# Attention scores ahead of the next group's query products on TensorE

## The reference

```
q = (u @ w_qg)[:, :1024] -> (group 4, head 4, token 512, 64) * 64**-0.5
for each block of 128 tokens:
    sc  = q @ kc.T                      # 31 compressed keys
    pc  = masked_softmax(sc)            # over the compressed keys
    ssel = q @ selected keys.T          # 16 >= 8 blocks, so all causal keys
    ps  = masked_softmax(ssel)
    sw  = q @ window keys.T             # window 512, so all causal keys too
    pw  = masked_softmax(sw)
    o   = gate0 * pc @ vc + gate1 * ps @ vs + gate2 * pw @ vw
y = o @ w_o
```

## Time and profile before

| what | value |
|---|---|
| median of 3 runs | 1482.14 us |
| the profiled execution, its time | 1483.61 us |
| the profiled execution, its span | 1481.9 us |
| attention loop on TensorE | about 800.7 to 1035 us of the span |
| PE busy over the span | 1299.8 us (88%) |
| mean granted TensorE clock | 0.935 |

### The profile page before, as it was taken

One profiled execution on the slowest core, in us unless ns is written; L12 is line 12 of the kernel. 1 busy time (PEld: TensorE's weight loads), 2 busy tenths in 40 slices (PEclk: granted clock), 3 DMA queues, 4 the chain that ended last, 5 costly groups with the idle time before them and its releaser, 6 DMA issues.

```text
span 1481.9 us, 18499 instructions
## 1 busy us (share of the span) xinstructions
PE 1299.8 (88%) x6655; PEld 1012.4 (68%) x6655; DVE 1086.3 (73%) x1201; ACT 770.5 (52%) x998; POOL 303.3 (20%) x344
## 2 busy tenths in 40 slices
PE   1399997949999999988989999999985999999985
PEld 0277775747777777747986677675774777777762
DVE  5648683868888888857984666655368888888867
ACT  0322321317777777754443555567142777777760
POOL 3011111421000000026101554445151100000020
PEclk9999998859999999999979999999966999999998
DMA  8657775319999999961621332330623999999972
GB/s 305 235 165 244 268 247 216 128 57 340 404 376 390 394 386 381 387 229 43 219 62 68 103 101 86 100 115 22 226 112 131 386 382 386 384 384 386 392 285 86
DMA packets 107568, 356.07 MB, mean 240 GB/s; under 512 B 8034, under 2 KB 16446, under 8 KB 107470
## 3 DMA queue, kind: packets, MB, share of 16 engines
q1 hardware_dynamic: 82984, 269.52, 48.4%
q0 software_dynamic: 19952, 69.83, 13.6%
q10 hardware_dynamic: 4566, 15.84, 2.6%
HBM read 330.99 MB, written 25.21 MB: 240 GB/s over the span
## 4 chain that ended last, share of the span: by engine, by line
PE 39%; issue 33%; DVE 14%; ACT 6%; DMA 5%; POOL 3%; ACTq 0%; DVEq 0%; POOLq 0%
PE bank L233 8%; PE bank L234 7%; PE bank L235 7%; DVE acc L361 3%; PE bank L1934 2%; PE bank L1952 2%; DMA xg<-scratch_u,tok 2%; POOL prob L2169 2%; PE bank L894 1%; PE bank L1922 1%; ACT w_hi L1107 1%; DMA ada<-in_ada_w_dram 1%; POOL xg L1043 1%; PE bank L1923 1%; DMA rows<-scratch_mods 1%
## 5 line engine op out<-in xcount | busy, mean ns | idle before, releaser
L1113 DVE TENSOR_TENSOR w_lo<-raw,w_hi 128x2048 fp32r<-128x2048 f32 x189 | 436.9, 2316 | 71.6 <-ACT w_hi L1107 71.2
L1107 ACT ACTIVATE w_hi<-raw 128x2048 fp32r<-128x2048 f32 x189 | 362.5, 1919 | 85.6 <-PE bank L235 75.1
L233 PE MATMUL bank<-w_lo,xe_hi 128*128 128x512 f32 x512 | 212.6, 415 | 10.5 <-DVE xe_lo L1070 10.4
L235 PE MATMUL bank<-w_hi,xe_hi 128*128 128x512 f32 x512 | 204.5, 399 | 0.0
L234 PE MATMUL bank<-w_hi,xe_lo 128*128 128x512 f32 x512 | 204.3, 399 | 0.0
L228 DVE TENSOR_TENSOR w_lo<-raw,w_hi 128x2048 fp32r<-128x2048 f32 x37 | 87.1, 2358 | 109.9 <-ACT w_hi L223 109.7
L1043 POOL DMA_INDIRECT xg<-scratch_u,tok x32 | 38.2, 1193 | 555.9 <-DVE tok L1037 555.3
L223 ACT ACTIVATE w_hi<-raw 128x2048 fp32r<-128x2048 f32 x37 | 70.5, 1910 | 134.5 <-PE bank L235 125.7
L233 PE MATMUL bank<-u_lo,w_hi 128*128 128x512 f32 x288 | 119.9, 416 | 11.3 <-DVE q L1839 9.3
L2169 POOL TENSOR_SCALAR prob<-prob,rsum,gates 128x512 f32<-128x512 f32 (+3 forms) x128 | 108.5, 862 | 100.4 <-DVE rsum L2137 100.2
L233 PEld LDWEIGHTS bank<-w_lo,xe_hi 128*128 128x128 f32 x512 | 97.6, 191 | 40.3 <-issue 11.9
(11 more groups left out here) (297 smaller groups left out, 2467.7 us busy)
## 6 DMA issues: line engine op xcount, KB each, us to landing
raw<-in_w_gu_dram SPq DMA_DIRECT2D x128, 1024.0 KB, 8.2
raw<-in_w_down_dram SPq DMA_DIRECT2D x64, 1024.0 KB, 8.6
ada<-in_ada_w_dram POOLq DMA_DIRECT2D x64, 512.0 KB, 5.4
ada<-in_ada_w_dram SPq DMA_DIRECT2D x32, 512.0 KB, 3.8
scratch_y<-ye ACTq DMA_DIRECT2D x30, 512.0 KB, 7.5
raw<-in_conv_w_in_dram SPq DMA_DIRECT2D x12, 1024.0 KB, 9.6
raw<-in_w_kv_dram SPq DMA_DIRECT2D x6, 1024.0 KB, 8.0
rows<-scratch_mods POOLq DMA_DIRECT2D x10, 512.0 KB, 7.7
```

The source lines that it names most:

```text
L233: nc.tensor.matmul(o, lh, rl, start=start, stop=False)
L235: return nc.tensor.matmul(o, lh, rh, start=False, stop=stop)
L1107: nc.scalar.activation(w_hi[:, hslot, :], raw[:, slot, :], ACT.Copy).then_inc(hi_done, 1)
L1113: nc.vector.tensor_tensor(w_lo[:, slot, :], raw[:, slot, :], w_hi[:, hslot, :].bitcast(F32), ALU.subtract).then_inc(lo_done, 1)
```

## The change

In `attention_pe`, the loop over a step's units that calls `scores_pe` moves above the block that calls `q_part_pe`. Nothing else is different; no instruction is added or removed.

```diff
@@ -2032,11 +2032,11 @@
             pe.wait_ge(vcz_made, 1 + GQA)
             for s in range(NS):
                 g, j = divmod(s, NSG)
+                for u in units_of(s):
+                    scores_pe(pe, u)
                 if g + 1 < NKV and j % 5 != 4 and j < 9:
                     for k in range(2):
                         q_part_pe(pe, g + 1, j // 5, 2 * (j % 5) + k)
-                for u in units_of(s):
-                    scores_pe(pe, u)
                 for n, h in mod_half_at(s):
                     mod_half_pe(pe, n, h)
                 if s >= 1:
```

## The result

The changed kernel took 1471.48 us, median of 7 runs (1469.34 to 1475.84). The kernel before had 1482.14 us over 7 runs, those with the change among them (1477.17 to 1487.15). The ratio is 0.9935 with a 95% interval of 0.9915 to 0.9955, so the gain is 9.6 us, between 6.7 and 12.6 (the two medians alone lie 10.7 apart). Forecast were 5.2 us gained and 1476.9 us, with a range down to 1472.9. One later execution of the kernel before was slow, 2544.11 us at a granted clock of 1.00, and is left out of all comparisons.

The account below looks back on a forecast made before the run. TensorE, busy 88% of the span, was taken as the bound in attention except at a few waits. Terms: 4.8 + 2.6 + 0.5 - 2.7 = 5.2 us gained, 1482.14 - 5.2 = 1476.9 us, range 1472.9 to 1480.6.

Parts of the forecast that it names:

- Step 5, the cover: Step 5, groups 0 to 2: scores fill TensorE's wait before the query products, idle 3.1 to about 1.5 us; 4.8 us gained.
- Step 5, the clock: Step 5, groups 0 to 2: two of three clock falls behind the wait go; 2.6 us gained, bounds 0 and 3.9.
- The start: First compressed scores, group 0: idle time grows from 0.72 to 2.1 us, clock may fall; 2.7 us lost, bounds 0 and 3.7.
- The wait for GpSimd in step 9: Group 0, step 9: the transposes' 0.53 us wait for step 8's scaling goes; 0.5 us gained.
- Other steps … Zero: Steps 1 to 3, 6 to 8 and compressed scores of groups 1 and 2: zero, the latter bounded by 0 and 0.7 us.
- the rival in which the falls grow: Longer low-clock stretches behind compressed scores, groups 0 to 2: 8.7 us lost against 5.3 gained, 1485.5 us; chance 0.04.
- The experts: After attention: forecast to move as one piece; rival that layer B's weight loads wait the gain away, 1482.1 us, chance 0.05.
- The rule of the Trainium skill: Would leave all clock terms out, making the sum 5.3 us gained; the prediction kept them, and they set the range's width.

Follow-up runs that it names:

- the kernel with the filler: Kernel before, with step 5's scores run once more as a thrown-away filler ahead of the query products in groups 0 to 2; ratio 0.9971.
- step 5 alone: Kernel before, with scores moved ahead of the query products only in step 5 of groups 0 to 2; ratio 0.9934.
- everything but step 5: Kernel before, with scores moved ahead of the query products in every step except step 5; ratio 1.0002.
- the filler at the start: Changed kernel plus six dense products, never read, in the idle time ahead of the first compressed scores; ratio 0.9940 against the kernel before.
- the kernels that change single groups: Kernel before, with scores ahead in step 5 of groups 1 and 2 only, or of group 0 only; loop 224.64 and 228.62 us.

## Why the prediction was right and wrong

*Step 5, the cover: right.* Forecast 3 x 1.60 = 4.8 us, idle time 1.5 us; measured 1.41 us of idle time and 3 x 1.51 = 4.5, from the kernel with the filler. No wait for `att_exp` took its place, and L1839 did not come later.

*Step 5, the clock: right in kind, too small in this pair.* Forecast 2.6 of at most 3.9. All three falls went: 8.83 - 4.5 = 4.3 us. The prediction compared waits of 0.72 and 3.1 us and left out the one of 2.33 between them, behind which the clock was low too (0.57 in 814 to 818 us). Over three profiles of each kernel step 5 shrank by 32.57 - 24.69 = 7.9, so the clock's part was 3.4 on average. Of all kernels here, the clock fell behind an idle time of 3.1 us in 14 of 18 places, and behind one of 1.4 us in 6 of 39.

*The start: right in two profiles of three.* Forecast 2.7 lost, bounds 0 and 3.7; the three profiles of the change have 2.5, 4.6 and 2.5 us over the 19.12 of before, since in one of them the clock fell a second time. That the compressed scores are late by the clock is shown by the filler. But the loss did not reach the time: the kernels without it were no faster.

*The wait for GpSimd in step 9: gone, as forecast, 0.5 us.* That one in step 6 of group 1 would grow from 0.17 to 0.65 us was not foreseen.

*"Other steps … Zero": this step failed.* The prediction took the compressed scores of groups 1 and 2 as unchanged, with at most 0.7 us lost. It had the rows of their falls in hand and used them for the start's loss and for the rival in which the falls grow, not as a term that could go away. They went: 4.13 us in this pair, and 4.0 on average over three profiles of each kernel (24.79 against 20.80 for both groups). Not all of this is the clock: in group 1, 0.7 us (10.97 against 10.29) is a wait for GpSimd that the new order covers, so the prediction, which bounded the order's effect here by 0 and 0.7 us lost, had its sign wrong too; for group 2 no profile separates the two. Of what the forecast missed in the loop (10.3 - 5.2 = 5.1 us), 4.1 is this and 1.7 is the clock at step 5. Less the longer wait in step 6 and a few tenths elsewhere, that closes. It does not need the new order at step 0: step 5 alone brought the loop as far down (L 221.98 and 222.07). The size of this term in one pair of profiles is partly luck, as L of the kernel before alone differs by 3.5 us between its profiles.

*The experts: right.* In this pair the time outside the loop differs by 1.0 us, so nothing was waited away.

*The rule of the Trainium skill.* The page "TensorE: Matmul & The Clock Gate", Part 1, advises not to fit to a count of slow matmuls and puts the warm-up at under 1% of a typical kernel. The rows agree with the second: all clock terms together, at most 4.3 + 4.1 - 2.5 = 5.9 us, are 0.4% of the span. The first part is borne out too, as one program has several patterns of falls. But a forecast without them would have left out about half of what the loop gained here.

What stays open is what decides whether the clock falls behind the compressed scores. It is neither the order at step 0 alone (falls with both), nor dense products among the narrow ones, nor the new start alone. The two together were not taken apart. With the scores ahead both at the start and at step 0 (the change three times, everything but step 5, and the filler at the start), 9 of 10 places in groups 1 and 2 had no fall; with the scores ahead at step 0 but not at the start, 1 of 10; with the order of before at step 0, 3 of 20. It also goes with what happened earlier in the loop, as the kernels that change single groups suggest. Why all three profiles of the full change had no fall there was not settled.

## What to carry to other kernels

If an engine waits in program order at an instruction that needs a late result, look at what stands behind it and needs nothing: here 12 matmuls moved in each of 3 steps are the whole gain, and the 21 other steps of the same edit gave nothing that could be measured. A wait on TensorE costs its length and often a stretch at half clock behind it, so price both where a wait goes and where the edit uncovers one, and enter every stretch at the lower clock near the edit with both signs, since falls tens of us away from an edit can come or go with it.

## What the runs showed of the hardware

One and the same program shows two or more patterns of clock falls: L of the kernel before was 232.33, 228.81 and 232.32 us, with three, one and three falls in step 5. Its times spread from 1474.1 to 1485.5 us over 29 runs, so one execution of each kernel cannot tell changes of 5 us. Filling 1.6 us of each of three waits with work whose result is thrown away made the kernel 4.3 us faster. The clock was at 1.2 GHz during narrow matmuls (32 columns) that kept TensorE busy by its record: in the kernel before 6.80 of 6.80 us at 0.50 in group 1, with no wait of TensorE listed since the one that ended at 855.80 us, and with the change 6.10 of 6.10 us at 0.58, there behind 2.2 us of idle time. Dense products between the narrow ones did not prevent it in the one kernel that had them.
